# Encoder block on eight cores: a ring of eight squared-ReLU pieces for FF1's last three tiles, pieces tracked by halves, and FF2's last tile by column halves

## What is computed

```
x1  = LN1(ALPHA * x + mix_out)                     (attention and gating give mix_out)
h   = square(relu(x1 @ w_ff1))                     (S, 4096)
out = LN2(ALPHA * x1 + h @ w_ff2)                  (S, 1024)
```

## Time and profile before

| | |
|---|---|
| median of 3 runs | 2793.95 us (2792.86 to 2794.05) |
| the profiled execution | 2794.41 us |
| its span on the slowest core (core 2) | 2792.8 us |
| spans of the eight cores | 2781.2 to 2792.8 us |
| TensorE busy on core 2 | 2645.5 us, 95% of the span |
| last matmul of the front (mix, L760) | 1718 us |
| last matmul of FF1 | 1903 us |
| FF2 | to the end |

### The profile page before, as it was taken

How to read it: one execution, slowest core, us unless ns; L and a number is a source line. 1 busy time by engine, 2 the same in 40 slices (tenths; PEclk the granted TensorE clock), 3 DMA queues, 4 the chain that set the end, 5 groups by cost and what they waited for, 6 DMA issues and landing times.

```text
span 2792.8 us, 57164 instructions; the slowest of 8 cores (2781.2 to 2792.8 us)
## 1 busy us (share of the span) xinstructions
PE 2645.5 (95%) x20844; PEld 1706.4 (61%) x20844; DVE 1491.9 (53%) x2558; ACT 1072.5 (38%) x2241; POOL 955.4 (34%) x661
## 2 busy tenths in 40 slices
PE   4689999999999999999999998899999999999996
PEld 2357777777677777777777676775444444444442
DVE  5876776767777777677767574111222221233222
ACT  4445555555555555555555452221111110111111
POOL 0333333333343333343333334222343322443332
PEclk8789999999999999999999999999999999999998
DMA  9744323423333433333333225663443434543431
GB/s 264 220 128 111 103 80 100 110 88 96 99 102 86 107 95 92 100 103 88 107 97 102 80 92 133 156 189 121 151 164 138 147 141 153 177 159 136 157 106 76
DMA packets 110134, 345.81 MB, mean 124 GB/s; under 512 B 11680, under 2 KB 11680, under 8 KB 99744
## 3 DMA queue, kind: packets, MB, share of 16 engines
q1 hardware_dynamic: 72208, 199.27, 20.6%
q10 hardware_dynamic: 17920, 100.67, 10.7%
q0 software_dynamic: 19728, 42.21, 10.0%
HBM read 250.10 MB, written 134.22 MB: 138 GB/s over the span
## 4 chain that ended last, share of the span: by engine, by line
PE 78%; ACT 6%; DVE 6%; issue 4%; DMA 4%; POOL 2%; DVEq 0%; ACTq 0%; SPq 0%; POOLq 0%
PE psum L836 27%; PE psum L804 23%; PE psum L760 8%; PE psum L659 4%; PE psum L673 4%; PE psum L675 4%; DMA hsc<-arena 2%; PE psum L729 2%; ACT L678 1%; PE psum L716 1%; DVE arena L689 1%; DMA arena<-w_gu 1%; PE psum L665 1%; PE psum L667 1%; PE psum L754 1%
## 5 line engine op out<-in xcount | busy, mean ns | idle before, releaser
L804 PE MATMUL psum<-arena 128*128 128x256 bf16 x8192 | 999.6, 274 | 15.8 <-ACT arena L648 9.8
L836 PE MATMUL psum<-arena 128*128 128x512 bf16 x4096 | 891.5, 379 | 4.5 <-POOL arena L858 2.3
L804 PEld LDWEIGHTS psum<-arena 128*128 128x128 bf16 x8192 | 773.2, 98 | 163.0 <-issue 56.1
L836 PEld LDWEIGHTS psum<-arena 128*128 128x128 bf16 x4096 | 399.5, 98 | 491.0 <-issue 16.6
L809 POOL TENSOR_TENSOR arena<-arena 128x512 bf16<-128x512 f32 x256 | 268.9, 1050 | 699.8 <-ACT arena L807 402.1
L807 ACT ACTIVATE arena<-psum 128x512 f32<-128x512 f32 x512 | 302.8, 592 | 370.7 <-PE psum L804 341.1
L774 POOL TENSOR_TENSOR arena<-arena 128x1024 f32<-128x1024 f32 x128 | 309.2, 2415 | 301.4 <-DVE arena L771 273.3
L843 DVE SCALAR_TENSOR_TENSOR arena<-psum,arena 128x512 f32<-128x512 f32 x128 | 88.3, 692 | 593.2 <-PE psum L836 521.6
L646 ACT ACTIVATE arena<-arena 128x1 f32<-128x1 f32 x320 | 93.3, 293 | 782.4 <-DVE arena L849 660.1
L856 POOL TENSOR_TENSOR arena<-arena 128x1024 f32<-128x1024 f32 x62 | 145.7, 2351 | 558.9 <-ACT arena L853 558.9
L809 DVE TENSOR_TENSOR arena<-arena 128x512 bf16<-128x512 f32 x256 | 214.7, 838 | 173.4 <-ACT arena L807 90.5
(11 more groups left out here) (82 smaller groups left out, 2182.4 us busy)
## 6 DMA issues: line engine op xcount, KB each, us to landing
hsc<-arena SPq DMA_DIRECT2D x256, 256.0 KB, 2.5
arena<-hsc ACTq DMA_DIRECT2D x64, 1024.0 KB, 5.3
arena<-x SPq DMA_DIRECT2D x64, 512.0 KB, 5.5
x1s<-arena SPq DMA_DIRECT2D x64, 512.0 KB, 3.4
arena<-x1s ACTq DMA_DIRECT2D x32, 1024.0 KB, 6.1
out<-arena SPq DMA_DIRECT2D x32, 1024.0 KB, 4.1
arena<-xt POOLq DMA_DIRECT2D x64, 256.0 KB, 5.2
arena<-w_ff SPq DMA_DIRECT2D x32, 512.0 KB, 5.5
```

The source lines that it names most:

```text
L804: R.pe(lambda e, fc=fc, ph=ph, z=z: [e.matmul(ph.ap[:, z * 256:(z + 1) * 256], lhsT=w1q[fc // 4].ap[:, c, (fc % 4) * 128:(fc % 4 + 1) * 12 ...
L836: R.pe(lambda e, s_=s_, q=q: [e.matmul(ps[s_][hf].ap, lhsT=hb[fc // 16].ap[:, fc % 16, s_ * 128:(s_ + 1) * 128], rhs=w2c[fc // 4].ap[:, fc ...
```

## The change

Four things, in the diff's order. (1) For tiles 29, 30 and 31 FF1 writes its pieces into a ring of eight buffers `hx00` to `hx13` of 1024 columns, which lie in the space of `hT[1]`, in place of the two `hst`. A `memset` of one column on VectorE, ahead of tile 29, stands for all the trackers that lie under `hT[1]`; `hT[1]` in turn depends on the ring's pieces, so its first load (tile 1) waits for the stores of tile 31. (2) For every tile the two halves of a piece are tracked apart. (3) The planner is told 680 elements in place of 512 for VectorE's square. (4) Tile 31 of FF2 has a function of its own, `ff2_last`: the four accumulations (s_, hf) are recorded one after the other in steps of 4 matmuls, each has its eviction and `bn_stats` recorded behind it, the LayerNorm is two passes of VectorE on 512 columns with no pass on ScalarE, and each quarter (256 KB) has its own store, on SP's queue for hf = 0 and on ACT's for hf = 1.

```diff
--- before.py
+++ after.py
@@ -340,6 +340,7 @@
 
 def build_nc(T=SEQ, dbg=False, verbose=False):
     NB = T // 128
+    NHXT = 3
     LAG0, LAG1, GROW = 2, 6, 2
     W2G = 2
 
@@ -474,6 +475,8 @@
         A.cover([b_.lt for b_ in x1T[i]])
     rl = [A.buf(f"rl{i}", F32, [512]) for i in range(2)]
     hst = [A.buf(f"hst{i}", BF16, [1024]) for i in range(2)]
+    hst2 = [[Buf(h_.ap[:, k * 512:(k + 1) * 512], f"hh{i}_{k}") for k in range(2)] for i, h_ in enumerate(hst)]
+    A.cover([b_.lt for h2 in hst2 for b_ in h2])
     W1OFF = A.off
     w1q = [A.buf(f"w1q{q}", BF16, [8, 512]) for q in range(8)]
     FIRST_END = A.off
@@ -489,12 +492,26 @@
         ap = A2.alloc(dtype, shape)
         return Buf(ap, name, extra=A.under(*A2.last))
 
+    hxw = []
+    hxg = LT("hxg")
     w2c = [over(f"w2c{q}", BF16, [4, D]) for q in range(8)]
     NHT = 3
     hT = [None] * NHT
     x1r = []
     hT[0] = [over(f"hT0_{g}", BF16, [16, 256]) for g in range(2)]
-    hT[1] = [over(f"hT1_{g}", BF16, [16, 256]) for g in range(2)]
+    hT[1] = []
+    hx, hx2 = [], []
+    for g in range(2):
+        ap = A2.alloc(BF16, [16, 256])
+        t = Buf(ap, f"hT1_{g}", extra=A.under(*A2.last))
+        hxgate_w = t.extra
+        flat = ap.rearrange("p a b -> p (a b)")
+        for k in range(4):
+            hx.append(Buf(flat[:, k * 1024:(k + 1) * 1024], f"hx{g}{k}"))
+            hx2.append([Buf(hx[-1].ap[:, z * 512:(z + 1) * 512], f"hx{g}{k}{z}") for z in range(2)])
+            t.extra = t.extra + [b_.lt for b_ in hx2[-1]]
+        hT[1].append(t)
+        hxw.extend(hxgate_w)
     x1r.append(over("x1r0", F32, [2, D]))
     assert A2.off <= A_END, (A2.off, A_END)
     G2 = Buf(G1.ap, "G2", extra=[G1.lt])
@@ -793,9 +810,15 @@
         R.tag = f"ff1{i}"
         R.at(2 * i + lag(i) + V_FF, 2.0, 72)
         xt = x1T_all[i % NX1]
+        if i == NI - NHXT:
+            R.dve(lambda e: e.memset(nmr1[0].ap, 0.0), [], [hxg, nmr1[0]] + hxw, 1)
         for g in range(8):
-            hs = hst[hn[0] % 2]
-            hkey = f"hst{hn[0] % 2}"
+            if i >= NI - NHXT:
+                j = hn[0] % len(hx)
+                hs, h2, hkey, hg = hx[j], hx2[j], f"hx{j}", [hxg]
+            else:
+                j = hn[0] % 2
+                hs, h2, hkey, hg = hst[j], hst2[j], f"hst{j}", []
             hn[0] += 1
             for k in range(2):
                 ph, r_ = psH[k], rl[k]
@@ -806,10 +829,10 @@
                         start=(c == 0), stop=(c == 7)) for c in range(8)], [w1q[g]] + w1p[4 * g:4 * g + 4] + x1T[i % NX1], [ph], [256] * 8)
                 R.act(lambda e, ph=ph, r_=r_: e.activation(out=r_.ap, in_=ph.ap, func=AF.Relu), [ph], [r_], 512)
                 eng = R.dve if k == 0 else R.pool
-                eng(lambda e, hs=hs, r_=r_, k=k: e.tensor_tensor(out=hs.ap[:, k * 512:(k + 1) * 512], in0=r_.ap, in1=r_.ap,
-                                                                 op=ALU.mult), [r_], [hs], 512)
+                eng(lambda e, hk=h2[k], r_=r_: e.tensor_tensor(out=hk.ap, in0=r_.ap, in1=r_.ap, op=ALU.mult),
+                    [r_] + hg, [h2[k]], 512 if k else 680)
             R.dma("sp", lambda e, hs=hs, g=g: e.dma_start(out=hsc[i, :, g * 1024:(g + 1) * 1024], in_=hs.ap),
-                  [hs], [h_lt[i][g]], hkey, 262144)
+                  h2, [h_lt[i][g]], hkey, 262144)
 
     def load_w2(q, after):
         R.dma("pool", lambda e: e.dma_start(out=w2c[q].ap.rearrange("p c n -> p (c n)"), in_=w_ff2[q]),
@@ -852,13 +875,47 @@
                                                         op0=ALU.mult, op1=ALU.mult), [mvB[p], rstdB[p]], [nmrB[p]], 1)
             R.act(lambda e, s_=s_, p=p: e.activation(out=yo.ap[:, s_, :], in_=yo.ap[:, s_, :], func=AF.Identity,
                                                      bias=nmrB[p].ap, scale=rstdB[p].ap), [yo, nmrB[p], rstdB[p]], [yo], 1024)
-            aff = R.dve if i == NI - 1 else R.pool
+            aff = R.pool
             aff(lambda e, s_=s_: e.tensor_tensor(out=yo.ap[:, s_, :], in0=yo.ap[:, s_, :], in1=G2.ap, op=ALU.mult),
                 [yo, G2], [yo], 1024)
             aff(lambda e, s_=s_: e.tensor_tensor(out=yo.ap[:, s_, :], in0=yo.ap[:, s_, :], in1=B2.ap, op=ALU.add),
                 [yo, B2], [yo], 1024)
         R.dma("sp", lambda e: e.dma_start(out=out[i * 256:(i + 1) * 256, :].rearrange("(s p) d -> p s d", p=128), in_=yo.ap),
               [yo], [], f"out{i % 3}", 1048576)
+
+    def ff2_last(i):
+
+        R.tag = f"ff2{i}"
+        R.at(1000.0 + i, 1.0, 50)
+        hb, yo = hT[i % NHT], x1r[i % 3]
+        ps = psY[i % 2]
+        for s_ in range(2):
+            p = s_
+            yh = [Buf(yo.ap[:, s_, hf * 512:(hf + 1) * 512], f"yh{s_}{hf}", extra=[yo.lt] if s_ == 0 and hf == 0 else []) for hf in range(2)]
+            for hf in range(2):
+                sl = slice(hf * 512, (hf + 1) * 512)
+                for q in range(8):
+                    R.pe(lambda e, s_=s_, q=q, hf=hf: [e.matmul(ps[s_][hf].ap, lhsT=hb[fc // 16].ap[:, fc % 16, s_ * 128:(s_ + 1) * 128],
+                                                                rhs=w2c[fc // 4].ap[:, fc % 4, hf * 512:(hf + 1) * 512],
+                                                                start=(fc == 0), stop=(fc == 31)) for fc in range(q * 4, q * 4 + 4)],
+                         [hb[q // 4], w2c[q]], [ps[s_][hf]], [512] * 4)
+                R.dve(lambda e, s_=s_, hf=hf, y_=yh[hf]: e.scalar_tensor_tensor(
+                    out=y_.ap, in0=ps[s_][hf].ap, scalar=1.0 / ALPHA, in1=y_.ap, op0=ALU.mult, op1=ALU.add),
+                    [ps[s_][hf], yh[hf], yo], [yh[hf]], 512)
+                R.dve(lambda e, hf=hf, p=p, y_=yh[hf]: e.bn_stats(out=stB[p].ap[:, hf * 6:(hf + 1) * 6], in_=y_.ap), [yh[hf]], [stB[p]], 512)
+            R.dve(lambda e, p=p: e.bn_aggr(out=mvB[p].ap, in_=stB[p].ap), [stB[p]], [mvB[p]], 52)
+            rsqrt(mvB[p].ap[:, 1:2], mvB[p], epsB, 1.0, lnvB[p], rstdB[p])
+            for hf in range(2):
+                R.dve(lambda e, hf=hf, p=p, y_=yh[hf]: e.scalar_tensor_tensor(
+                    out=y_.ap, in0=y_.ap, scalar=mvB[p].ap[:, 0:1], in1=G2.ap[:, hf * 512:(hf + 1) * 512],
+                    op0=ALU.subtract, op1=ALU.mult), [yh[hf], mvB[p], G2], [yh[hf]], 512)
+            for hf in range(2):
+                R.dve(lambda e, hf=hf, p=p, y_=yh[hf]: e.scalar_tensor_tensor(
+                    out=y_.ap, in0=y_.ap, scalar=rstdB[p].ap, in1=B2.ap[:, hf * 512:(hf + 1) * 512],
+                    op0=ALU.mult, op1=ALU.add), [yh[hf], rstdB[p], B2], [yh[hf]], 512)
+                R.dma("sp" if hf == 0 else "act", lambda e, s_=s_, hf=hf, y_=yh[hf]: e.dma_start(
+                    out=out[i * 256 + s_ * 128:i * 256 + (s_ + 1) * 128, hf * 512:(hf + 1) * 512], in_=y_.ap),
+                    [yh[hf]], [], f"outl{s_}{hf}", 262144)
 
 
     fn = 0
@@ -895,7 +952,10 @@
     for i in range(NI):
         if i + 2 < NI:
             ff2_load(i + 2)
-        ff2(i)
+        if i < NI - 1:
+            ff2(i)
+        else:
+            ff2_last(i)
 
     R.emit(nc, es)
     if verbose:
```

## The result

The changed kernel is slower. Its median is 2835.8 us against 2794.0, the ratio **1.0135 [1.0118, 1.0152]**, which is 38 us (ratios are turned into time with 2794 throughout); the forecast was 2776.2, and its range ended at 2785. (The ratio leaves disturbed runs out, the median does not.) The profiled execution took 2834.07 us.

What follows compares the result with a forecast made beforehand. TensorE, busy 95% of the span, was taken as the bound. On core 2, -1.8 - 2.3 - 1.7 - 11.9 = -17.7 us gave 2776.7 against the profiled 2794.4, 2776.2 for the median; range 2768 to 2785.

Steps and rivals of the forecast that it cites:

- Part 3: Front, planner's price of VectorE's square 680 instead of 512: reorders every stream; taken as 0, 6 us either way.
- Rival C: Front: new order delays attention's VectorE work, TensorE waits longer; up to 6 us gives 2782, 24 us more 2800; chance 0.13.
- Part 2: Halves of a piece tracked apart: GpSimd's square may start 0.8 us earlier; taken as 0, between +1 and -3 us.
- Part 1: Last three FF1 tiles, eight-buffer ring: store waits go, -1.8 us on core 2, -4.8 on core 0.
- Part 4: Last tile of FF2 in column halves: on core 2 wait -2.3, clock -1.7, tail -11.9 us.
- (c): Tail behind the last matmul: 8.2 us against 20.1, -11.9 us, bounds -11 and -12.5.
- The forecast's side sum: By the skill's DMA figures the last quarter's store takes 2.6 us, the whole 4.4: 0.2 us less gain than by rows.
- (a): TensorE's wait at 2757, ahead of the last steps, goes: 13 small steps, 11.1 us against 10.85; -2.3 us.
- rival B: Last tile gets its tail but not its feed, 2780, or `hT[1]`'s late load stops TensorE, 2783; chance 0.20.
- (b): Last matmuls behind the wait at 2757: without idle time the clock does not fall, -1.7 us on core 2, 0 on core 0.
- Rivals A and D: A: front's new order gains too, 2770, chance 0.17. D: last tile's s_ halves still end together, 2781, chance 0.04.
- The marks given for a wrong forecast: Front busy time over 6 us from 1490, a TensorE wait for a load behind FF1, a tail over 10 us.

Runs made afterwards that it cites:

- the last experiment: Kernel before plus `ff2_last`, 204 words free ahead of `hT[1]`, ReLU ahead of the Ln in 4 blocks; no ring, no halves, price 512: 2773.9 us, 0.9927.

## Why the prediction was wrong, step by step

**Part 3, the planner's 680: this step failed.** It was put at 0 with 6 us either way, "a tenth of 59.7", because "no row says what a new order gives". It costs 1.06%, 30 us, alone and 51 in the whole (with the halves' 14 to 18 that go with it). The bound had no row under it: 59.7 us is what TensorE *idles*, and a new order can add idle time that the old trace does not hold, and slower matmuls behind it. The row that could have warned stood in the waits of before, second behind the earlier trace rows: `L804 <- L648`, 9.5 us in 8 cases, at 1.2 us a case. The step that was left out was to ask what keeps that number at 8, and the answer is in the streams (4 blocks of 40 without the ReLU), which the planner writes without a chip. The argument that 863 ns is "nearer to what is seen" was of no use: a planner's price is worth what the order it leads to is worth. The planner counts the table load too (1283 ns); what it had wrong is when the ReLU can start. On the chip its bank was full about 2 us before the load at 1015.05; playing `schedule` for a block of that kind shows it ready only when the Ln is due.

**Rival C** had the mechanism's kind (the planner's order makes the front idle more) and its deciding point, 17.7 us more idle time; measured are 31 on core 4 by the named waits. It had the place wrong, attention's L722, which grew by 4 us only (0.9 by the price, 3.0 by the halves), and 0.04 for a cost beyond 23 us.

**Part 2, the halves: wrong in the new order.** "0, between +1 and -3" holds with 512 (0.999 [0.9967, 1.0013]). With 680 it costs 0.5 to 0.7%. The prediction took a false wait for something that can only be in the way; here it kept two engines apart in the blocks of the front, though how that becomes TensorE's loss stays open.

**Part 1, the ring: mechanism right, balance wrong.** The square's waits went as said. The -1.8 us did not arrive: the price named as "at worst 2 us", ReLUs behind ACT's queue waiting for piece 3, is 2.38 us of TensorE with the ring alone and 3.39 in the changed kernel, with 2.8 us of slower matmuls behind it, so the bound was too small and should not have been put at 0. The forecast of no harm behind FF1 held: no wait of TensorE for a load beyond 1 us there.

**Part 4.** (c) The tail is 8.46 us (forecast 8.2): evictions, passes (1.42 and 1.41 us for two) and store as priced. The forecast's side sum with 4.4 us for the whole store and 2.6 for a quarter has the wrong sign: 1.8 us saved is 0.2 more than the 1.6 of the rows, not less. The forecast did not use it. (a) The wait shrank to 1.12 us and did not go. The 10.85 us from the eviction to the free tracker are there again (2799.22 to 2810.07), and so are the 13 small steps (11.39 us from 2797.56 on). What was overlooked is that the eviction starts 1.66 us after these steps do. It waits for GpSimd's offset of tile 30's first half (`<-POOL arena L881`), since `yo` is tracked as one buffer, so tile 30 ending 2.6 us earlier does not bring its eviction forward by as much. This is the margin of 0.25 us that rival B doubted. That the rest hangs on the shared tracker is shown by the last experiment, which takes it away. (b) The clock: on all eight cores of the changed kernel the last matmuls behind the 1.12 us take 13.97 us, the full clock. Before, behind 2.32 us, they took 15.53 to 15.66 us on five of the eight cores, core 4 among them, and 13.97 on three. So the 1.7 us came in.

**The sum without part 3.** The kernel with 512 measures 0.9952, -13 us, against the forecast of -17.7; of the 4 to 5 us that are missing 1.8 are the ring's, 1.1 the wait's, and the rest lies inside the interval of 4 us either way. **Rivals A and D** did not happen: no gain in the front, and s_ = 0 ends 7.7 us ahead.

The marks given for a wrong forecast worked: "busy time from 100 to 1650 us that differs by more than 6 us" is what shows, by 39 as recorded, and by 31 when only named waits are counted.

## What to carry to other kernels

Where a scheduler writes the streams, a changed price is a changed program: compare the old and the new order of every engine before costing it at nothing, and look for a cheap operation that frees a matmul's bank and has slipped behind one that waits for another engine or loads a table. A dependency that computes nothing may still keep two engines apart, and taking it away cost 0.5 to 0.7% in one order and nothing in another, so price it in the order that it will run in. The end of a kernel, behind its last matmul, is where a gain could be priced from rows and arrived almost as priced (11.7 us of 11.9). And a wait of TensorE can cost more than its length: look at the mean length of a matmul record as well as at the idle time.
